# One-core decoder block: loads, norms and column sums ahead of the second norm in another order, and one product moved behind transposes

## The reference

```
mod = silu(c) @ ada_w + ada_b;  sh1, sc1, gt1, sh2, sc2, gt2 = split(mod, 6)
h = rms_norm(x, pre_g1) * (1 + sc1) + sh1
q, k, v, z_u, z_v, g_attn, g_gmlp = split(h @ w_in)
y_attn = attention(q, k, v, rel_bias)            # 8 heads of 64, causal, bucketed bias
y_gmlp = gelu(z_u) * (W_s @ layer_norm(gelu(z_v)) + b_s)
y = (sigmoid(g_attn)*(y_attn @ w_a) + sigmoid(g_gmlp)*(y_gmlp @ w_g)) @ w_out
x = x + gt1 * rms_norm(y, post_g1)
h = rms_norm(x, pre_g2) * (1 + sc2) + sh2        # "the second norm"
q = h @ w_query; 16 best of 128 x 128 expert pairs for each of 8 heads and token
y = sum over picks of gate * gelu(h . u_e) * v_e # 16384 experts u, v of 1024
out = x + gt2 * rms_norm(y, post_g2)
```

## Time and profile before

| what | us |
|---|---|
| median of 3 runs (1685.68 to 1686.49) | 1686.26 |
| the profiled execution's own time | 1687.21 |
| its span in the trace | 1685.5 |
| PE busy in the span | 1520.3 |
| DVE busy in the span | 1361.4 |

### The profile page before, as it was taken

One profiled execution on the slowest core, in us unless ns is written; L12 is line 12 of the kernel. 1 busy time (PEld: TensorE's weight loads), 2 busy tenths in 40 slices (PEclk: granted clock), 3 DMA queues, 4 the chain that ended last, 5 costly groups with the idle time before them and its releaser, 6 DMA issues.

```text
span 1685.5 us, 25524 instructions
## 1 busy us (share of the span) xinstructions
PE 1520.3 (90%) x7943; PEld 1303.4 (77%) x7943; DVE 1361.4 (81%) x2701; ACT 657.4 (39%) x1101; POOL 823.4 (49%) x800
## 2 busy tenths in 40 slices
PE   4999799997978656768999999999999999999996
PEld 3677566684747545567999999999999999999995
DVE  5776544352579999848999999999999999999998
ACT  3332245421137663333443433434334334344343
POOL 1000100001029876637666676666666666766662
PEclk7999899998989857989999999999999999999998
DMA  9974121232000007899999999999999999999992
GB/s 348 357 267 159 64 73 50 100 129 74 1 1 1 1 13 227 256 299 407 406 403 385 382 382 388 383 379 392 383 379 387 388 379 384 386 383 384 384 387 103
DMA packets 193019, 448.90 MB, mean 266 GB/s; under 512 B 30699, under 2 KB 80131, under 8 KB 192716
## 3 DMA queue, kind: packets, MB, share of 16 engines
q1 hardware_dynamic: 136780, 243.65, 40.7%
q0 software_dynamic: 56192, 204.66, 31.0%
HBM read 424.57 MB, written 23.10 MB: 266 GB/s over the span
## 4 chain that ended last, share of the span: by engine, by line
PE 76%; DVE 12%; DMA 5%; issue 3%; POOL 2%; ACT 2%; SPq 1%; POOLq 0%; DVEq 0%; ACTq 0%
PE bank L818 13%; PE bank L993 9%; PE bank L992 9%; PE bank L991 9%; PE bank L1014 7%; PE bank L1012 7%; PE bank L1013 7%; PE bank L757 4%; PE bank L1004 3%; PE bank L1005 3%; PE bank L918 2%; DMA w_scratch<-staged 2%; DMA u_raw<-u_by_key 1%; DMA ring<-w_in 1%; POOL hot L692 1%
## 5 line engine op out<-in xcount | busy, mean ns | idle before, releaser
L991 PE MATMUL bank<-h_hi,u_hi 128*128 128x320 f32 x1024 | 316.5, 309 | 11.8 <-DVE u_lo L1807 11.8
L992 PE MATMUL bank<-h_lo,u_hi 128*128 128x320 f32 x1024 | 316.9, 310 | 0.0
L993 PE MATMUL bank<-h_hi,u_lo 128*128 128x320 f32 x1024 | 316.9, 309 | 0.0
L668 POOL DMA_INDIRECT v_rows<-v_exp,small x192 | 261.6, 1363 | 91.5 <-POOL small L664 51.8
L668 POOL DMA_INDIRECT u_rows<-u_exp,small x192 | 241.6, 1258 | 92.5 <-POOL small L664 51.2
L1323 ACT ACTIVATE v_hi<-v_raw 128x1024 fp32r<-128x1024 f32 x128 | 135.8, 1061 | 241.6 <-PE bank L1014 126.4
L991 PEld LDWEIGHTS bank<-h_hi,u_hi 128*128 128x128 f32 x1024 | 192.8, 188 | 17.2 <-issue 12.0
L1014 PE MATMUL bank<-v_hi,g_both 128*128 128x512 f32 x512 | 204.5, 399 | 0.0
L1012 PE MATMUL bank<-v_hi,g_both 128*128 128x512 f32 x512 | 203.6, 398 | 0.0
L1013 PE MATMUL bank<-v_lo,g_both 128*128 128x512 f32 x512 | 203.4, 397 | 0.0
L1807 DVE TENSOR_TENSOR u_lo<-u_raw,u_hi 128x1024 fp32r<-128x1024 f32 x128 | 157.4, 1231 | 55.2 <-ACT u_hi L1316 55.2
(11 more groups left out here) (247 smaller groups left out, 2940.4 us busy)
## 6 DMA issues: line engine op xcount, KB each, us to landing
u_raw<-u_by_key SPq DMA_DIRECT2D x128, 512.0 KB
v_raw<-v_exp SPq DMA_DIRECT2D x128, 512.0 KB
ada_blk<-ada_w SPq DMA_DIRECT2D x24, 1024.0 KB, 10.7
w_row<-w_scratch SPq DMA_DIRECT2D x128, 160.0 KB
ring<-w_in SPq DMA_DIRECT2D x18, 1024.0 KB, 5.1
w_scratch<-staged SPq DMA_DIRECT2D x2, 8192.0 KB, 30.8
xr<-x SPq DMA_DIRECT2D x8, 512.0 KB, 6.1
ring<-w_branch SPq DMA_DIRECT2D x4, 1024.0 KB, 5.1
```

Of the source, the lines that this page charges most:

```text
L668: pool.indirect_dma_start(out=rows[:, s], out_offset=None, in_=table, in_offset=bass.IndirectOffsetOnAxis(ap=ix[:, s:s + 1], axis=0))\
L991: pe.matmul(o, u_hi[:, r, k], h2_hi[:, k], start=(k == 0), stop=False)
L992: pe.matmul(o, u_hi[:, r, k], h2_lo[:, k], start=False, stop=False)
L993: last = pe.matmul(o, u_lo[:, r, k], h2_hi[:, k], start=False, stop=(k == KD - 1))
```

## The change

- SP: the third block of `ada_w` in order (b = 1) goes to the ring slot of `BLOCKS[1]`, so it is issued with no wait; the fourth waits for one summed block, not two; the fifth moves ahead of `BLOCKS[1]`, which now waits for three.
- ACT: squares of x ahead of the copies of `ext`; the scaling of x (`nat`) moves from DVE to ACT. POOL: the norms of x ahead of the bias store; the load of `flipped` waits for two summed blocks; the layer norm's `v_rs` ahead of the wait for all row sums and of `wsT`.
- PE: four bias products, both column sums, four bias products. For heads 4 to 7 the last job (j = 3, six matmuls) of the pair runs behind the transposes.
- DVE: `with_gain` row by row, right behind the `plus_bias` that completes a row; `low(21)` behind the first `zv_normed`.
- Second norm: squares, norms and steps of x in the order x0, h2 0, x1, h2 1; ACT's `x_squares(1)` behind the first `h2_across`.
- Ahead of the gate loop: `divide(3)`, the clearing of `acc0` and three copies into `gate_by` go behind DVE's loop; `expd[3]` moves to 174.5 KB, and ACT no longer waits for the last picks. An iota and its cast that nothing read are gone.

```diff
-BIAS_FIRST = [("bt", h) for h in range(6)] + [("col", 1), ("bt", 6), ("col", 3), ("bt", 7)]
+BIAS_FIRST = [("bt", h) for h in range(4)] + [("col", 1), ("col", 3)] + [("bt", h) for h in range(4, H)]
-NORMS = [(0, t) for t in range(NT)] + [(1, 0), (1, 1), (2, 0), (2, 1), (1, 2), (1, 3), (2, 2), (2, 3)]
+NORMS = [(0, t) for t in range(NT)] + [(1, 0), (2, 0), (1, 1), (2, 1), (1, 2), (1, 3), (2, 2), (2, 3)]
-        expd = [at(f"expd{e}", kb, [P, P]) for e, kb in enumerate((91.5, 103, 108.5, 109))]
+        expd = [at(f"expd{e}", kb, [P, P]) for e, kb in enumerate((91.5, 103, 108.5, 174.5))]
+        def ada_place(n):
+            return (2, 0) if n == 2 else (n, 0) if n < 2 else ((n + 1) % 2, (n - 1) // 2)
+        def ada_rows(n):
+            r = ada_place(n)[0]
+            return ring[:, SLOT[BLOCKS[1]]] if r == 2 else ada_blk[:, r]
@@ sync, load_ada
-                if n >= 2:
-                    sp.wait_ge(chunks_summed, n - 1)
+                r, turn_of = ada_place(n)
+                if turn_of:
+                    sp.wait_ge(chunks_summed, max(m for m in range(n) if ada_place(m)[0] == r) + 1)
@@ sync
             load(BLOCKS[0], 1)
+            load_ada(4)
+            sp.wait_ge(chunks_summed, 3)
             load(BLOCKS[1], 0)
             load(BLOCKS[1], 1)
...
-            load_ada(4)
             load_ada(5)
@@ gpsimd
+            for t in range(NT):
+                norm(0, t)
             stored(pool, ("ext", 0), ("ext", 1))
             pool.dma_start(bias_dram, ext).then_inc(bias_out, 16)
-            for t in range(NT):
-                norm(0, t)
             pool.wait_ge(bias_out, 16)
+            pool.wait_ge(chunks_summed, 2)
             pool.dma_start(flipped, ...)
             pool.dma_start(ln_row, ...)
-            multiplied(pool, *group("ada"))
-            ... (load and mask of wsT)
             for t in range(NT):
                 pool.wait_ge(v_var, t + 1)
                 ...
+            multiplied(pool, *group("ada"))
+            ... (load and mask of wsT)
@@ tensor, pair(p, some=range(4)) runs the jobs in some
                 for p in pairs_before(h):
-                    pair(p)
+                    pair(p, range(4) if pairs_behind(h) else range(3))
                 ... (transposes)
                 for p in pairs_behind(h):
                     pair(p)
+                if not pairs_behind(h):
+                    for p in pairs_before(h):
+                        pair(p, (3,))
@@ scalar
+            for t in range(NT):
+                act.wait_ge(x_in[t], 16)
+                squares(0, t, xr[:, t, :], junk)
             for f in range(2): ... (ext)
             for t in range(NT):
-                act.wait_ge(x_in[t], 16)
-                squares(0, t, xr[:, t, :], junk)
+                act.wait_ge(rstd_ready, t + 1)
+                act.activation(nat[:, t, :], xr[:, t, :], ACT.Copy, scale=rstd(0, t)).then_inc(xn_ready, 1)
...
             squares_of(1, 0, nat[:, 0, :], junk2)
+            x_squares(0)
             mixer_out(1)
             squares_of(1, 1, nat[:, 1, :], junk2)
-            x_squares(0)
-            x_squares(1)
...
                 h2_across(t)
+                if t == 0:
+                    x_squares(1)
...
-            act.wait_ge(picks_ready, NT)
@@ vector
-            for t in range(NT):
-                dve.wait_ge(rstd_ready, t + 1)
-                dve.tensor_scalar(nat[:, t, :], xr[:, t, :], rstd(0, t), None, ALU.mult).then_inc(xn_ready, 1)
...
                     plus_bias(ada_behind(p - 1))
+                if ada_behind(p - 1) in (8, 9, 11):
+                    with_gain({8: 2, 9: 4, 11: 5}[ada_behind(p - 1)])
...
             zv_normed(0)
-            zv_normed(1)
-            zv_normed(2)
             low(21)
-            zv_normed(3)
-            ... (with_gain of rows 2, 4 and 5)
+            for t in range(1, NT):
+                zv_normed(t)
             low(22)
...
             x_step(0)
+            h2_step(0)
             x_step(1)
-            h2_step(0)
             h2_step(1)
...
-            divide(3)
-            link(dve.memset(acc0, 0.0))
-            dve.wait_ge(picks_ready, NT)
             (idx_by from picks; wait ex_in; idx_by from ex_picks; no copies to gate_by here)
             with dve.Fori(EARLY // 4, ALL_GROUPS // 4) as m: ...
+            divide(3)
+            link(dve.memset(acc0, 0.0))
+            dve.wait_ge(picks_ready, NT)
+            (the three copies into gate_by)
```

More of the change, by code:

```diff
@@ L399, in build @@
         ada_b2_in = sem("ada_b2_in")
-        ada_in = [[sem(f"ada_in{r}_{half}") for half in range(2)] for r in range(2)]
+        ada_in = [[sem(f"ada_in{r}_{half}") for half in range(2)] for r in range(3)]
         hot_in, rel_in, rel_mask, bias_out, bias_in, keys_in = (
@@ L508, in load_ada @@
                 n = ADA_ORDER.index(b)
-                if n >= 2:
-                    sp.wait_ge(chunks_summed, n - 1)
+                r, turn_of = ada_place(n)
+                if turn_of:
+                    sp.wait_ge(chunks_summed, max(m for m in range(n) if ada_place(m)[0] == r) + 1)
                 for half in range(2):
                     rows = slice(4 * half, 4 * half + 4)
-                    sp.dma_start(ada_blk[:, n % 2, rows], w_src("ada", b)[:, rows]).then_inc(ada_in[n % 2][half], 16)
+                    sp.dma_start(ada_rows(n)[:, rows], w_src("ada", b)[:, rows]).then_inc(ada_in[r][half], 16)
             for t in range(NT):
@@ L638, in _ @@
             pool.dma_start(ln_row, ln_gb.partition_broadcast(P)).then_inc(ln_in, 16)
+            for t in range(NT):
+                pool.wait_ge(v_var, t + 1)
+                link(pool.tensor_scalar(v_ms(t), mv(t)[:, 1:2], 1.0, EPS, ALU.mult, ALU.add))
+                pool.tensor_tensor(v_rstd(t), v_ms(t), mhalf, ALU.pow).then_inc(v_rs, 1)
             multiplied(pool, *group("ada"))
@@ L791, in columns, with pair @@
                 full(last, "col", b)
-            def pair(p):
+            def pair(p, some=range(4)):
                 block, q = PAIRS[p]
@@ L808, in pair @@
                 for j, job in enumerate(jobs):
+                    if j not in some:
+                        continue
                     o = start(*job) if first else bank(*job)
@@ L821, in pair @@
                         full(last, *job)
-                if not last_pair:
+                if not last_pair and 3 in some:
                     last.then_inc(pairs_used, 1)
@@ L1409, in plus_bias, with with_gain @@
                 dve.tensor_tensor(half, o[:, :], half, ALU.add).then_inc(free("ada", b), 1)
-            def with_gain(row, gain, one, by=ALU.add):
-                link(dve.scalar_tensor_tensor(mod(row), mod(row), one, gain, by, ALU.mult))
+            def with_gain(row):
+                n, one, by = {2: (0, 0.0, ALU.add), 4: (1, 1.0, ALU.add), 5: (2, math.sqrt(D), ALU.mult)}[row]
+                stored(dve, ("ada", 2 * row), ("ada", 2 * row + 1))
+                dve.wait_ge(gains_in, 16)
+                dve.scalar_tensor_tensor(mod(row), mod(row), one, gains[:, n], by, ALU.mult).then_inc(mods_ready, 1)
             def chunks(b):
@@ L1505, in _ @@
             zv_normed(0)
-            zv_normed(1)
-            zv_normed(2)
             low(21)
-            zv_normed(3)
-            stored(dve, *group("ada"))
-            dve.wait_ge(gains_in, 16)
-            for row, gain, one in ((2, gains[:, 0], 0.0), (4, gains[:, 1], 1.0)):
-                with_gain(row, gain, one)
-            with_gain(5, gains[:, 2], math.sqrt(D), ALU.mult)
-            dve.nop().then_inc(mods_ready, 1)
+            for t in range(1, NT):
+                zv_normed(t)
             low(22)
@@ L1801, in _ @@
                     ins.then_inc(hots_dve, 1)
+            divide(3)
+            link(dve.memset(acc0, 0.0))
+            dve.wait_ge(picks_ready, NT)
+            for to, of in mine:
+                ins = dve.tensor_copy(gate_by[:, :, to], by_four[2][:, :, of])
+            ins.then_inc(ex_placed, 1)
+            dve.tensor_copy(gate_by[:, :, 1:4:2], by_two[1]).then_inc(ex_placed, 1)
             def u_low(j, q):
```

20 lines of the change are left out of this document (4 added, 16 removed).

## The result

The changed kernel takes **1660.61 us** (median of 4 runs, 1658.70 to 1662.45); the kernel before took 1686.22 beside it (4 runs, 1685.68 to 1686.49). The ratio is 0.985, with a 95% interval of 0.9838 to 0.9861, so 25.6 us are gone where 28.45 were forecast. The profiled execution took 1661.41, its span is 1659.7 against 1685.5. PE does the same work in less time; what went is idle time and time at the lower clock.

The account below looks back on a forecast made before the run. PE, busy 1520.3 of 1685.5 us, was taken as the bound, with gains in its idle stretches on one chain before the expert loop. Terms 3.3+12.2+2.7+8.6+1.65 = 28.45 us gave a median of 1657.8, range 1654.5 to 1666.

Parts of the forecast that it names:

- Stage A: Start of the kernel up to the first pairs: weights land earlier and DVE sums start earlier, pair 0 3.3 us earlier.
- DVE no longer scales x and can start when the first half has landed: Ahead of pair 0: DVE's first column sum starts at 13.8 us, its second ends 3.1 us earlier.
- No stall: Between pairs 1 and 2: sums 3 and 4 are there after four bias products, 48.2 against 48.1 us, with no slack.
- Pair 2 starts 3.3 earlier: Pair 2 comes 3.3 us before 59.83, not more, since ACT still copies the last bias row before `rows_high(2)`.
- Stage B: Around pairs 20 and 21: PE's 9.35 us hole goes, 24 matmuls stay at the higher clock, `mix` starts 12.2 us earlier.
- the other three `zv_normed` take 5.9: DVE ahead of `mix`: these end at 179.0 us, when pair 21 ends, so `mix` starts at 179.1.
- Stage C: Heads 4 to 7: six matmuls fill holes behind transposes; heads 5 to 7 gain 3.0 us, head 4 loses 0.3, sum 2.7.
- Stage E: Second norm: transposes follow the mixer's products at once, `query` takes 16.16 us, not 16.61, and ends 8.6 us earlier.
- Stage F: Ahead of the gate loop: only indices and the wait for `ex_picks` remain; loop starts 1.65 us earlier, bounds 0.6 and 2.1.
- The loop stage: Expert loop, 721.8 to 1650 us, PE busy for 914 of 928: nothing in it edited, its 928 us unchanged.
- Rival 4: Expert loop paced by DMA swallows the gains, 0.22 us a block over 128 blocks; chance 0.02.
- rival 3: More than the sum: PE stays warm in stages A and E, 1 to 3 us more, 1655 to 1657; chance 0.11.

Follow-up runs that it names:

- c1: The changed kernel run and profiled once more, unedited: 1659.61 us.
- x6: The changed kernel with DVE scaling x again ahead of the column sums, the late load of `flipped` kept: 1661.58 us.
- x7: The changed kernel with ACT making `rows_high(2)` after the fourth and fifth bias rows, the sixth only behind it: 1657.99 us.
- x4: The changed kernel with each pair of heads 4 to 7 whole ahead of the transposes again: 1660.88 us.
- x13: The changed kernel with five edits together: x7, x8, x9, x12, and head 4's pair whole ahead of its transposes: 1646.15 us.
- x3: The changed kernel with the second norm's squares, norms and steps back in the old order: 1669.97 us.
- x5: The changed kernel with `divide(3)`, the clearing and the copies ahead of the gate loop again: 1661.87 us.
- x9: The changed kernel with the gathers' indices, and their wait for `ex_picks`, moved behind the gate loop: 1659.76 us.
- x8: The changed kernel with the weights of row block 5 applied behind the second norm's v steps instead of before them: 1660.93 us.
- x2: The changed kernel with three `zv_normed` ahead of `low(21)` again, POOL's scalars staying early: 1665.53 us.
- x12: The changed kernel with the second norm's transposes for tiles 0 and 1 inside the mixer's output products, ACT copying them before that product: 1653.34 us.

## Why the forecast was right, and which terms were off

**Stage A** was forecast at 3.3 and gave 3.35 in the first profile, 2.3 in c1. That the first fits to 0.05 is luck of the clock: it is 2.89 at pair 0, less 0.69 and 0.10 up to pair 2, plus 1.25 behind it. The step "DVE no longer scales x and can start when the first half has landed" is right in its end and wrong in its cause for the larger part (x6): by the traces some 1.8 us came through ACT's squares and 0.75 through the move of the scaling. The landing of the first half of `ada_w` then set the start; it came at 13.6 to 14.7, with the 13.8 I worked out amid them. "No stall" on the column sums and on `flipped` (issued at 26.81, asked for at 45.73) held. "Pair 2 starts 3.3 earlier" did not: 2.1, and 1.0 in c1. The mis-sized parts are pair 0 (2.9 and 2.4) and the length of pairs 0 and 1, which I had as unchanged and which ran 0.69 and 1.26 longer at the lower clock. The wait behind ACT's copies of bias rows was as forecast, 3.18 against 3.08: it had been there before, and I left it (x7: 2.7 of it go).

**Stage B**, 12.2 forecast, 11.3 and 11.4 measured. The mechanism held: no hole, pair 21 at full clock. The mis-sized step is "the other three `zv_normed` take 5.9": one of their operations runs beside POOL's mask and takes 0.93 more. I had noted that the last `v_normed` was within 0.2 of being late and priced nothing on it.

**Stage C**, 2.7 forecast, 2.2 measured. Heads 5 to 7 give 0.94, 0.87 and 0.90, not 1.0 each, and head 4 loses 0.5, not 0.3. x4 and x13 confirm both signs.

**Stage E**, 8.6 forecast, 8.52 measured; x3 shows that it is the order. That it fits to 0.1 is partly luck: a query behind transposes and a wait of 2.1 to 2.3 takes 14.5 or 16.2 by the execution, and c1 gives 10.14. Between 16.16 and 16.6 I chose rightly, since 16.6 came in none of the 20 queries of this kind, but the choice left out the 14.53; behind the wait of 8.60 it was 16.61 before and 15.99 in x3.

**Stage F**, 1.65 forecast, 1.05 measured, with another 0.43 in the picks that I had not foreseen and do not explain. The landing of `ex_picks` took 2.14 from its issue, not 1.8, and 0.56 lay between the landing and the loop, not 0.3. The 1.8 was right for the kernel before (1.79); in all thirteen profiles since, x5 with its old order ahead of the loop included, the last quarter took 2.12 to 2.42. What stretches it no run shows. x9 shows that this wait held the loop's start: without it the loop starts 0.97 behind the issue.

**The loop stage** was forecast unchanged. Its 0.97 more is not an effect of the change: over 13 profiles of this kernel and its variants the stage took from 964.7 to 966.0, and once 967.4, with before's 965.06 amid them. Rival 4, that the loop swallows the gain, is out. Of rival 3 (PE stays warm) there is something in executions such as c1, whose profile is 27.6 under before's.

## What to carry to other kernels

Where a chain of holes sets the time, sum the holes by releaser, then ask of each engine's list what will be next on the path when the hole is gone: here it was a mask on POOL, and a wait behind copies on ACT that had stood on the path all along. Compare stages between profiles rather than totals: x4, x8 and x9 moved their stage by 1.1 to 2.2 us and their medians by less than 1, which is also how far apart the two medians of the changed kernel lie. And where PE waits for a copy of its own transposes, put the transposes inside the product ahead, not behind it: that was the largest single gain left (7.3 us), because it removed the waits and the clock's fall behind them.

## What the hardware showed that I had not expected

**The clock behind a short wait differs from one execution to the next.** Behind the same transposes and the same waits, the 128 matmuls of a query took 14.53 us in some executions and 16.16 in others. Of the 20 queries in the ten profiles with the new order of the second norm and the transposes behind the product, 5 took 14.53 (one each in c1, x4 and x7, two in x2), the others 16.16. In c1 both lengths stand in one execution. With the wait gone (x12, x13) all four took 14.45 by the timeline, with the eight transposes still there; x12's granted clock was 1.00 from 61.83 to 457.78 without a break. From the gate's transposes to head 0's it is alike: 10.9 us in eight of 14 profiles, before's among them, 12.5 in five, 14.1 in one. The windows show the clock at 0.50 there in one execution and 1.00 in another. The Trainium skill (TensorE: Matmul & The Clock Gate, Part 4: PE-mode transpose) says that transposes do not count as PE being busy in the same way. That fits x12, where eight transposes between matmuls left the clock at full, and the query behind transposes and a wait, where it fell; what decides between two executions no run here shows. The sets of runs were taken on different chips, so the chip may have a part in it: the four profiles of the first set all took 10.9 behind the gate's transposes, those of the two others took 10.9 twice, 12.5 five times and 14.1 once.

**What stays open.** x12's times lie within 1.54 us, about as they should if the queries made the spread. But x13's, with the same edit, lie 6.0 apart; the stretch behind the gate's transposes (up to 3.2) and the loop stage (1.3) do not make up all of it.
